# Expert weights loaded as rows of 8 KB, four consecutive rows to a partition, with gate and up in ring slots of their own

## What is computed

```python
def hierarchical_moe(h, w_group, b_group, w_router, b_router, w_gate, w_up, w_down):
    xf = h.reshape(t, d)                                   # 256 x 1024
    g_logits = (xf @ w_group + b_group)                    # 4 groups
    g_idx = jnp.argmax(g_logits, axis=-1)
    e_logits = (xf @ w_router + b_router)                  # 32 experts, 8 of the group count
    ...
    top_p, top_e = lax.top_k(e_probs, TOP_K)               # two experts for a token
    ...
    def expert_block(args):
        xblk, e = args
        hid = jax.nn.silu(xblk @ w_gate[e]) * (xblk @ w_up[e])
        return hid @ w_down[e]
    ...
    y = jnp.zeros((t, d), xf.dtype).at[sorted_tok].add(contrib)
```

## Time and profile before

| | |
|---|---|
| median of 3 executions | 2789.03 us (2778.6 to 2791.99) |
| the profiled execution, its own time | 2788.92 us |
| span of its profile | 2786.9 us |
| mean granted TensorE clock | 0.984 |
| PE busy | 2543.6 us, 91% of the span |
| DVE busy | 1236.3 us, 44% |
| ACT busy | 807.8 us, 29% |
| DMA packets | 388644, 716.22 MB, mean 257 GB/s |
| queue of SP | 384336 packets, 71.2% of 16 engines |

### The profile page before, as it was taken

One profiled execution on the slowest core, in us unless ns is written; L12 is line 12 of the kernel. 1 busy time (PEld: TensorE's weight loads), 2 busy tenths in 40 slices (PEclk: granted clock), 3 DMA queues, 4 the chain that ended last, 5 costly groups with the idle time before them and its releaser, 6 DMA issues.

```text
span 2786.9 us, 38902 instructions
## 1 busy us (share of the span) xinstructions
PE 2543.6 (91%) x15764; PEld 1786.2 (64%) x15765; DVE 1236.3 (44%) x2218; ACT 807.8 (29%) x1395; POOL 302.3 (11%) x390
## 2 busy tenths in 40 slices
PE   6998888988898988888899999899999999989998
PEld 3654332322495332332289898888989989888997
DVE  5553222111475221211154575556455457555645
ACT  2231000000142000000044444344444444444443
POOL 1210010000010010000000112240010011223101
PEclk8989999999998999999999999999999999999999
DMA  9979999999864999999947453343754645334372
GB/s 345 349 286 381 393 394 394 388 394 395 313 205 161 394 393 394 395 393 394 390 144 243 143 167 115 120 144 108 245 186 148 215 148 167 122 119 150 117 240 85
DMA packets 388644, 716.22 MB, mean 257 GB/s; under 512 B 18912, under 2 KB 192656, under 8 KB 382320
## 3 DMA queue, kind: packets, MB, share of 16 engines
q1 hardware_dynamic: 384336, 707.77, 71.2%
q10 hardware_dynamic: 2336, 3.52, 0.4%
q0 software_dynamic: 1792, 2.42, 0.3%
HBM read 709.69 MB, written 1.05 MB: 255 GB/s over the span
## 4 chain that ended last, share of the span: by engine, by line
PE 57%; DMA 26%; issue 7%; DVE 5%; POOL 3%; ACT 1%; SPq 1%; ACTq 0%; DVEq 0%; POOLq 0%
DMA ring<-in_e_w_down_dram 24%; PE w L756 17%; PE y L798 9%; PE w L760 9%; PE w L1022 5%; PE w L1008 3%; DMA ring<-in_ada_w_dram 2%; PE y L1048 2%; PE w L1271 2%; PE y L691 1%; POOL arena L2646 1%; SPq L665 1%; PE w L1256 1%; PE w L859 1%; DVE wsp L1380 1%
## 5 line engine op out<-in xcount | busy, mean ns | idle before, releaser
L1380 DVE TENSOR_TENSOR wsp<-ring,wsp 128x1024 fp32r<-128x1024 f32 x470 | 579.8, 1239 | 395.2 <-ACT wsp L1370 394.8
L756 PE MATMUL w<-hh,wsp 128*128 128x256 f32 x4832 | 639.1, 285 | 8.5 <-DVE wsp L1380 8.1
L756 PEld LDWEIGHTS w<-hh,wsp 128*128 128x128 f32 x4832 | 607.9, 192 | 29.5 <-issue 16.4
L1370 ACT CAST wsp<-ring 128x1024 fp32r<-128x1024 f32 x470 | 488.4, 1045 | 411.6 <-PE w L760 205.0
L1008 PE MATMUL w<-ring,arena 128*64 128x512 f32 x2048 | 470.8, 599 | 60.2 <-DMA ring<-in_e_w_up_dram 48.7
L1008 PEld LDWEIGHTS w<-ring,arena 128*64 128x64 f32 x2048 | 138.5, 136 | 356.7 <-issue 222.4
L760 PE MATMUL w<-hl,wsp 128*128 128x256 f32 x2416 | 339.7, 283 | 0.0
L760 PEld LDWEIGHTS w<-hl,wsp 128*128 128x128 f32 x2416 | 312.3, 192 | 0.0
L1022 PE MATMUL w<-ring,ht 128*64 128x512 f32 x1024 | 244.3, 600 | 55.2 <-DMA ring<-in_e_w_down_dram 54.0
L798 PE MATMUL y<-wsp,zsp 128*128 128x512 f32 x1104 | 267.1, 391 | 4.2 <-DVE wsp L1380 4.2
L2376 ACT ACTIVATE ht<-w 128x256 f32<-128x256 f32 x64 | 24.5, 383 | 786.0 <-PE w L1008 786.0
(11 more groups left out here) (331 smaller groups left out, 2281.9 us busy)
## 6 DMA issues: line engine op xcount, KB each, us to landing
ring<-in_e_w_gate_dram SPq DMA_DIRECT2D x256, 512.0 KB, 10.2
ring<-in_e_w_up_dram SPq DMA_DIRECT2D x256, 512.0 KB, 11.4
ring<-in_e_w_down_dram SPq DMA_DIRECT2D x128, 1024.0 KB, 13.7
ring<-in_ffn_in_dram SPq DMA_DIRECT2D x88, 1024.0 KB, 5.7
ring<-in_w_in_dram SPq DMA_DIRECT2D x50, 1024.0 KB, 5.2
ring<-in_ada_w_dram SPq DMA_DIRECT2D x48, 1024.0 KB, 11.2
ring<-in_ffn_out_dram SPq DMA_DIRECT2D x44, 1024.0 KB, 5.1
ring<-in_b_w_in_dram SPq DMA_DIRECT2D x12, 1024.0 KB, 12.0
```

What stands on the lines that cost most here:

```text
L756: pe.matmul(dst, a[:, kc * m:(kc + 1) * m], hh[:, kc, :], start=kc == 0 and j == 0, stop=False)
L1370: ac.copy(shaped(halves(i)[0], u.shape), u.cut(ring[:, u.piece % NSLOT, :])).then_inc(*mark("w_high", i))
L1380: ve.tensor_tensor(shaped(lo, u.shape), u.cut(ring[:, u.piece % NSLOT, :]), shaped(hi, u.shape).bitcast(F32), ALU.subtract).then_inc(*mark ...
```

## The change

A piece "up" is now 512 consecutive rows of gate, or of up, in one DMA of 1 MB: partition p gets the rows 4p to 4p + 3 of the block, which are one row of 8 KB in HBM. The pieces of an expert are gate and up of the first 512 rows, gate and up of the second, and two pieces "down" of 256 rows, two consecutive rows (8 KB) to a partition. PE waits for the gate and the up piece together and releases both when their eight matmuls are done. Since partition p of chunk kc now stands for another feature, the activations follow: `vh` and `vl` are written in that order (`by_four`, `in_chunks`), the scale and shift columns are permuted into `ab[:, 2:4, :]` by 16 small matmuls ahead of the router's shift and a copy on ACT, and silu and the product write their result with even and odd columns apart (`by_two`). Gathers wait for that copy.

```diff
@@ pieces
             elif w[0] == "up":
                 _, l, e_, h = w
+                g, u = divmod(h, 2)
                 piece_of[w] = len(pieces)
-                pieces.append({"parts": [
-                    (lambda r, q=q: r.rearrange("p (k u n) -> p k u n", k=2, u=2)[:, :, q, :],
-                     I[nm][l, e_, 256 * h:256 * h + 256, :].rearrange("(k p) n -> p k n", p=P))
-                    for q, nm in enumerate(("e_w_gate", "e_w_up"))], "units": []})
+                assert len(pieces) % 2 == u
+                src = I[("e_w_gate", "e_w_up")[u]][l, e_, 512 * g:512 * g + 512, :]
+                pieces.append({"parts": [(lambda r: r, src.rearrange("(p k) n -> p (k n)", p=P))], "units": [],
+                               "read": len(pieces) + 1 - u})
             elif w[0] == "down":
                 _, l, e_, h = w
                 piece_of[w] = len(pieces)
-                pieces.append({"parts": block(I["e_w_down"][l, e_, 256 * h:256 * h + 256, :], 2, D)[0], "units": []})
+                src = I["e_w_down"][l, e_, 256 * h:256 * h + 256, :]
+                pieces.append({"parts": [(lambda r: r, src.rearrange("(p k) n -> p (k n)", p=P))], "units": []})
@@
+        def by_four(a):
+            return a.rearrange("p (g q k) -> p g k q", g=2, k=4)
+        def in_chunks(a):
+            return a.rearrange("p (g k q) -> p g k q", g=2, k=4)
+        def by_two(a):
+            return a.rearrange("p (q c) -> p q c", c=2)
@@ sync_engine
                     else:
-                        sp.wait_ge(*at("ring_read", n - NSLOT))
+                        sp.wait_ge(*at("ring_read", pieces[n - NSLOT].get("read", n - NSLOT)))
@@ router_shift
                 pe.wait_ge(*at("route_v", "router", l))
+                o = WB[3][:, 64:80].rearrange("p (v g k) -> p v g k", v=2, g=2)
+                for j in range(4):
+                    for k in range(4):
+                        pe.matmul(o[32 * j:32 * j + 32, :, :, k], ident[:, k::4],
+                                  ab[:, 0:2, :].rearrange("p v (g j) -> p v g j", g=2)[:, :, :, j], start=True, stop=True)
                 o = WB[3][0:1, 0:40]
@@ up
-                    for h in range(4):
-                        np_ = piece_of["up", l, e_, h]
-                        pe.wait_ge(*at(f"ring{np_ % NSLOT}", np_))
-                        r4 = ring[:, np_ % NSLOT, :].rearrange("p (k u n) -> p k u n", k=2, u=2)
-                        for k in range(2):
-                            kc = 2 * h + k
+                    for h in range(2):
+                        for v in range(2):
+                            np_ = piece_of["up", l, e_, 2 * h + v]
+                            pe.wait_ge(*at(f"ring{np_ % NSLOT}", np_))
+                        s = np_ % NSLOT
+                        r4 = ring[:, s - 1:s + 1, :].rearrange("p u (k n) -> p k u n", k=4)
+                        for k in range(4):
+                            kc = 4 * h + k
@@ vector_engine, moe
-                    ve.tensor_tensor(vl[:, t, :], vv[:, t, :], vh[:, t, :].bitcast(F32), ALU.subtract).then_inc(*mark("route_v", "v_lo", l, t))
+                    ve.tensor_tensor(in_chunks(vl[:, t, :]), by_four(vv[:, t, :]), in_chunks(vh[:, t, :].bitcast(F32)), ALU.subtract).then_inc(*mark("route_v", "v_lo", l, t))
@@ gathered_half, gathered (DVE and ACT alike)
                     ve.wait_ge(*at("gathered", "half", l, part, q))
+                    ve.wait_ge(*at("route_s", "row", l))
...
-                                         ab[:, 0, kc:kc + 1], ab[:, 1, kc:kc + 1], ALU.mult, ALU.add).then_inc(
+                                         ab[:, 2, kc:kc + 1], ab[:, 3, kc:kc + 1], ALU.mult, ALU.add).then_inc(
@@ the product
-                        ve.tensor_tensor(hd[:, i, :], b[:, T:2 * T], hd[:, i, :], ALU.mult).then_inc(*mark("hd", l, e_))
+                        ve.tensor_tensor(hd[:, i, :].rearrange("p (c q) -> p q c", c=2), by_two(b[:, T:2 * T]),
+                                         hd[:, i, :].rearrange("p (c q) -> p q c", c=2), ALU.mult).then_inc(*mark("hd", l, e_))
@@ scalar_engine, moe
                 ac.wait_ge(*at("route_pe", "shift", l))
+                ac.copy(ab[:, 2:4, :].rearrange("p v k -> p (v k)"), WB[3][:, 64:80]).then_inc(*mark("route_s", "scale", l))
                 ac.copy(rb[:, l, :], WB[3][0:1, 0:40]).then_inc(*mark("route_s", "row", l))
...
-                    ac.copy(vh[:, t, :], vv[:, t, :]).then_inc(*mark("route_s", "v_hi", l, t))
+                    ac.copy(in_chunks(vh[:, t, :]), by_four(vv[:, t, :])).then_inc(*mark("route_s", "v_hi", l, t))
...
-                        ac.activation(hd[:, i, :], bank_of(("up", e_))[:, 0:T], ACT.Silu).then_inc(*mark("silu", l, e_))
+                        ac.activation(hd[:, i, :].rearrange("p (c q) -> p q c", c=2), by_two(bank_of(("up", e_))[:, 0:T]), ACT.Silu).then_inc(*mark("silu", l, e_))
```

More of the change, by code:

```diff
@@ L2333, in gathered_half @@
                     ac.wait_ge(*at("gathered", "half", l, part, q))
+                    ac.wait_ge(*at("route_s", "row", l))
                     for k in range(2):
@@ L2336, in gathered_half @@
                         ac.activation(xg[:, 0, kc, T * part:T * part + T], bank_of(("half", part, q))[:, T * k:T * k + T], ACT.Identity,
-                                      bias=ab[:, 1, kc:kc + 1], scale=ab[:, 0, kc:kc + 1]).then_inc(*mark("xg_s", l, "half", part, q))
+                                      bias=ab[:, 3, kc:kc + 1], scale=ab[:, 2, kc:kc + 1]).then_inc(*mark("xg_s", l, "half", part, q))
                 def gathered(g, kc):
```

33 lines of the change are left out of this document (17 added, 16 removed).

## The result

The changed kernel takes 2736.77 us (median of 4 executions, 2733.88 to 2743.17) where the kernel before takes 2785.07 beside it (4 executions, 2778.6 to 2791.99). The ratio is 0.983, interval 0.981 to 0.985: faster by 1.7%. The profiled execution took 2735.95 us, its span is 2733.9, 53.0 less than the span of before.

The account below looks back on a forecast made before the run. Transfers were taken to bound the two expert stages. Faster pieces less dry queue gained 56.1 us; less 1.0 for the router and 0.5 for silu and product, 54.6 from 2788.9 gave 2734.3 us, range 2722 to 2766.

Parts of the forecast that it names:

- Pace: Expert stages: 8 KB rows land a megabyte in 2.49 us, as ada_w's do; an expert takes 14.94, 1.01 less.
- Rivals 2 and 3: Expert stages: row size is not the cause, 2796 us (0.07); 8 KB partition step slows pieces, 2848 at 2.80 (0.05).
- the term of 62.9 us: Transfer gain at 0.168 us a megabyte: 32.3 us in the first expert stage, 30.6 in the second.
- Dry queue: Expert stages: transfers run out at expert 1, expert 17 and the second stage's start, since slots come free later.
- surcharge for the thin lead: Odd experts with gathering: refill leads the queue's end by 1.6 to 2.6 us; 0.1 us each charged, 2.5 in all.
- expert 1 of the first stage: Pair freed at 242.3, traffic at 243.9: queue dry 1.6 us, taken as 2.0 with SP's part.
- start of the second stage: Ring full, queue empty: first refill 1.73 us later, four pieces win back 0.7, so 1.1 net.
- expert 17, two stages: The residual adds 3.45 us before slots come free: queue dry 0.9 to 1.9 us, net 0.6 in each stage.
- T: Moment PE sees an expert's second down piece; the queue was to last to T + 14.1.
- Rival 1: Expert stages: longer PE waits drop the clock, some 1.7 us each, and the lead is lost: 2758 us; chance 0.24 (with slower pace).
- Router and hd: Router: small matmuls 2 us, low parts 10% longer, 1.0 lost in all; silu and product at expert 0, 0.5 in all.
- The last sign: The prediction is wrong if PE's start of the second stage moves from 877.51 by more than 2 us.

Follow-up runs that it names:

- e1: Changed kernel with gate and up in 2 KB rows again, same pieces, slots and waits: 2801.06 us, 1.006 of the kernel before.
- e2: Changed kernel with gate and up in 4 KB rows, two consecutive rows to a partition: 2748.34 us, 0.987 of the kernel before.
- e11: Changed kernel with eight ring slots in the expert stages and gate and up in 2 KB rows: 2778.15 us, 0.997 of the kernel before.
- e4: Changed kernel with contiguous reads and writes in the four operations that reorder activations: 2734.13 us, 0.981 of the kernel before.
- e3: Kernel before, with PE waiting for two pieces and releasing both after the second: 2790.91 us beside 2786.49, ratio 1.0026.
- e5: Changed kernel with eight ring slots in the expert stages, two in memory those stages don't use: 2728.8 us, 0.979 of the kernel before.
- e6: Changed kernel with the eight residual matmuls moved from expert 17 to expert 28: 2735.77 us, 0.982 of the kernel before.
- e9: Changed kernel measured once more, nothing altered, on the same chip as e10: 2738.0 us, 0.983 of the kernel before.
- e10: Changed kernel with eight ring slots in the expert stages, the spare two joined as a stage's fourth pair: 2724.99 us, 0.979 of the kernel before.
- e7: Changed kernel with eight idle matmuls ahead of the last expert's wait for weights, both stages: 2743.37 us, 0.984 of the kernel before.

## Why the prediction was right, and where it was off

The forecast was 2734.3 with 2722 to 2766 and faster by over 0.5% at 0.87; measured were 2736.8. The mechanism came as told: faster pieces, paid for in part by a queue that runs dry in a few places.

**Pace.** Taken: 2.49 us for a megabyte, 14.94 for an expert. Measured: 2.497, and 14.98. The choice to trust ada_w's row, which stands outside the stage but has the same form, was right, and e1, e2 and e11 show that it is the row size. The rule of the Trainium skill (DMA: Bandwidth & Descriptors, Specifications) that 512 B suffice does not hold here: 2 KB rows moved 397 GB/s and 8 KB rows 420 in otherwise equal kernels. Rivals 2 and 3 fell with that; the term of 62.9 us for both stages is 62.5.

**Dry queue.** Counted: 2.0, 1.1 and twice 0.6 net, and 2.5 as a surcharge for the thin lead, 6.8 in all. Measured: 10.8 more than before. This is the term that was mis-sized. By place, net of before, counted and then measured:

| | counted | measured |
|---|---|---|
| expert 1 of the first stage | 2.0 | 1.9 |
| start of the second stage | 1.1 | 2.7 |
| expert 17, two stages | 0.6, 0.6 | 1.6, 2.2 |
| expert 4, two stages | 0 | 1.0, 1.4 |
| 24 odd experts | 2.5 | none seen |

At expert 17 the step that failed is how long the queue lasts. T is 487.8; traffic was due at T + 15 to 16 and came at about 503, T + 15.3, but the queue ended at about 500.6, T + 12.8, not T + 14.1. The lag from a piece's last byte to PE's sight of it was taken too short. PE saw a pair at 482.50 and eight pieces stood behind it, due in sight by 482.5 + 8 x 2.497 = 502.5; the queue ended 1.9 us before that, where 0.8 was taken. Expert 4 was not foreseen: behind the matmuls of expert 3 PE has a combine and twelve gather matmuls between two releases, the same pile as at expert 17 with other work. I had asked where the residual stands and not where else the program puts so much between two releases. At the start of the second stage the refill came 1.7 us later, as counted, but the win that was set against it is not seen. What the surcharge paid for stood in a few places of 1 to 3 us.

**Clock.** Rival 1 said that the longer waits would drop the clock in experts 24 to 31. That happened, but not at each: of the five waits of 2.3 to 2.4 us there in the changed kernel, three were followed by a slow block (690, 1284 and 1314), two were not (660 and 1254). Its size was right, 8.78 us for 7.09, and its price was not: the next pair was not there anyway. The half clock cost nothing here, because a transfer ended the next wait.

**Router and hd.** Counted 1.0 and 0.5. The low parts took 65% more instead of 10%, the high parts twice their time, which is the upper end I had argued away; the small matmuls took 1.3 instead of 2. The layer's sum came to 0.2 us (30.3 to 30.5), because PE's wait before the second turn had room. At expert 0 the wait for the product went from 1.02 to 1.43 us in both stages, 0.8 for 0.5. e4 (2734.1 for 2736.8) is too near to tell any of it.

**The base.** The sum was made against 2788.9. The executions of before scatter by 14 us; their median beside the changed kernel is 2785.07, and beside the later runs 2785 to 2787: the profiled one was among the longer. Against it the gain is 52.1 us, 2.5 under the forecast of 54.6; against the median it is 48.3, 6.3 under. The stages agree with the second: 50.7 for a counted 56.1. That the forecast time came within 2.5 us is therefore luck in part: a gain told some 6 us too high was taken from a base some 4 us too long.

**The signs.** 420 GB/s and the pace came; the stages are 487 to 488 us for "some 480", and beside the places named there the queue was dry at expert 4 and at the start of the second stage, which only the sum had. The last sign was badly put: PE's start of the second stage did move, from 877.51 to 848.06, and by the prediction's own sum had to, since the first stage ends earlier. What should have been watched is the time between the stages, which moved by 0.7 us.

What stays open: why the first run (2 KB rows, six slots, pairs) had 24 us of dry queue where e3 (2 KB rows, six slots, pairs of half and half) had 14. The granted clock does not tell them apart: it is 0.98 in both stages of both (1.00 and 0.99 in the changed kernel). e11 only shows that in the first stage it ends with eight slots. Open too is what decides whether a wait of 2.3 us is followed by a lower clock.

## What to carry to other kernels

If a stage waits for one stream of transfers, look in the same trace for the same kind of transfer with longer rows, and price a megabyte of each: the difference per packet carries over into another stage. When such an edit also makes the unit of release coarser, walk through the program for every place where the consumer does the most between two releases, not only the one you know, and compare with the bytes that the ring holds at the new, faster pace; two more slots, in memory that the stage does not use, gave 13 us where moving single pieces of work gave none. And when slots are added, look in the trace for the first transfer into them: e5 had them on paper for 145 us before it used them.

## What the runs showed of the hardware

Rows of 2, 4 and 8 KB cost 2.71, 2.56 and 2.50 us for a megabyte on 16 DMA engines. A high part on ACT that reads every fourth float took 2.05 us instead of 1.05, a low part on DVE 1.94 instead of 1.18 (two in 3.87 and 2.35); writes in two interleaved runs with interleaved reads of PSUM took 625 ns instead of 384 on ACT and 618 instead of 425 on DVE. After waits of 2.3 us at the same place in the program TensorE's next 16 records took 5.35 us in four profiles of kernels with the 8 KB rows (the changed kernel, e5, e6, e9) and 3.65 in two (e4, e10). And the last ada piece, in work that no edit touches, was multiplied anywhere from 210.6 (e3) to 219.8 us (e7) on: a single profile of this kernel can be off by that much before the first expert begins, so stages have to be compared from their own start.
